# Expert weights of a two-layer MoE stack loaded as neighbouring rows per partition, with the fill of the modulation spread over single parts

## The chip, the cores and the metric

The kernel runs on one core of a Trainium2 chip. The metric is the device time of one execution in microseconds, from first instruction to last; less is better. Several executions are shown, and the median counts.

## What is computed

The reference chains two blocks on 256 tokens of width 1024, all in fp32. Cut to what matters:

```python
for l in range(2):                                   # first block
    x = x + 0.5 * swiglu(rmsnorm(x, norm_ffn1[l]), w_ffn1_in[l], w_ffn1_out[l])
    h = rmsnorm(x, norm_mix[l])
    x = x + mixing_sublayer(h, ...)                  # retention and forgetting attention, gated
    x = x + 0.5 * swiglu(rmsnorm(x, norm_ffn2[l]), w_ffn2_in[l], w_ffn2_out[l])
x = rmsnorm(x, norm_final)
...
for i in range(2):                                   # second block: x and 256 context tokens
    mod = silu(c) @ w_ada[i] + b_ada[i]              # also for c_ctx; shifts, scales, gates
    a = attention(x * (1 + sc1) + sh1)               # i == 0: window GQA, i == 1: differential
    x = layer_norm(ALPHA * x + g1 * a)
    h = x * (1 + sc2) + sh2
    s = sigmoid(h @ w_router)                        # 16 experts in 4 groups, top 2 of one group
    for e in range(16):
        y = (silu(h @ w_gate[e]) * (h @ w_up[e])) @ w_down[e]     # 1024 -> 512 -> 1024
        out = out + gates[:, e:e + 1] * y
    x = layer_norm(ALPHA * x + g2 * out)
```

Layer 0 of the second block routes 512 tokens (x and context), layer 1 only 256.

## The kernel before

The program is written by hand for each engine, in one order of stages: ffn0, mix0, ffn1, ffn2, mix1, ffn3 (the first block), then attention `qa`, `o0`, experts `m0` (4 tiles of 128 tokens), attention `qb`, `o1`, experts `m1` (2 tiles). Semaphores with named events (`pe.up(name)`, `q.wait_ge(*pe.at(name))`) tie the engines together.

**Weights.** A product in fp32 is made of three passes of PE over rounded halves: x_hi w_hi, x_hi w_lo, x_lo w_hi (`pe_gemm`, L334, L335, L336). `plan` cuts every weight into chunks of 1 MB (128 partitions x 2048 numbers) and each chunk into two parts of 128x1024. SP loads the chunks in program order into four buffers RAW (`load_chunks`, L300; `chunk_ap` gives the address). ACT rounds each part into HI (`hi_parts`, L268), DVE subtracts it from RAW into LO (`lo_parts`, L281, or L283 where a norm's gain is folded in), and five parts may be in flight. Both work four parts ahead of PE. A buffer is free for the next load once LO of both its parts is made.

In `chunk_ap` row k0*128 + k*128 + p of the weight goes to partition p ("(k p) c -> p k c"): a partition reads rows that lie 128 apart, each 512 columns or 2 KB in one packet. The x that is multiplied has the matching order, since PE turns blocks of 128 neighbouring columns.

**Experts.** In `pe_moe`, for each expert i: p of expert i-1 is turned, gate and up of expert i are multiplied (`a`, `b`, each 8 rows x 512 columns), the gathered x of i+1 is turned, and y of i-1 is made as two products of 512 columns from w_down, each by its own `pe_gemm` into its own PSUM bank. ACT makes silu(a) (L2036), and copies each y half out (L2049); DVE multiplies by b (L2244). POOL gathers the 128 tokens of an expert from HD by an indirect DMA (L2272); ACT's queue stores y to YD. The inputs h are made by `dve_modulate_folded` (L1342, L1344), two operations of 128x1024 for each tile of tokens, then stored to HD and turned for the router. Experts with over 128 tokens run again for the rest behind the loop (`pe_further` and its like): there PE multiplies RAW itself, unsplit (L1805, L1817). With these inputs two experts in each layer do.

**Fill.** The modulation `mod` needs w_ada, 96 parts for the whole program. Generators `pe_ada`, `act_ada`, `dve_ada` are stepped by `next(fill, None)` inside loops that have room: mix0 and mix1 (24 parts each) and the attention loop of qa (48 parts). One step brings two parts. In mix the loops have 5 steps in the retention part and 19 in and after the attention part, in qa there are 64 steps in the heads' loop (exp L1556) of which the first 32 work on scores of 512 columns and the last 32 on 256, with a copy on DVE (L1601) in every other step.

**Start.** For the first stage `act_ffn` and `dve_ffn` split the first weights (L537, L573) ahead of the norm; `act_norm` copies the turned x (L369) and squares x (L443).

## Time and profile before

| | before |
|---|---|
| runs shown, us | 2906.01, 2893.61, 2903.13 |
| median, us | 2903.13 |
| profiled execution: time, us | 2892.89 |
| profiled execution: span, us | 2891.1 |
| granted PE clock, mean | 0.916 |
| PE, PE weight loads, DVE, ACT busy | 89%, 70%, 61%, 50% |
| DMA moved | 575.90 MB, mean 199 GB/s |
| weight queue q1 | 249600 packets, 505.13 MB, 51.1% |

The shares are of the span. The span is what the profiler recorded from first to last instruction. PE is TensorE, DVE VectorE, ACT ScalarE, POOL GpSimd, SP the engine whose queue loads the weights. A share of a queue is the summed time of its packets over 16 DMA engines. The granted clock is a share of full speed (2.4 GHz): 1.00 or 0.50, or a mean of both over a stretch.

### The profile page before, as it was taken

To read this page: it belongs to the slowest core of one execution; us is meant where nothing else is said; L and a number is where in the kernel's file an instruction comes from. 1 tells how busy PE (TensorE), PEld (TensorE's weight loads), DVE (VectorE), ACT (ScalarE), POOL (GpSimd) and SP (SyncE) were. 2 spreads that over 40 slices of the span, in tenths; PEclk is the share of its full clock that TensorE was granted. 3 is DMA by queue.
4 is the path that set the end of the run, shared out by engine and by line. 5 is a ranking of instruction groups with operands and counts; after the bars stand their busy time and mean duration, and the time that the engine had idled before them with its cause. 6 is when DMAs were issued, how large, how long until landed. Compare 5 with 4: busy or idle time off the path is not lost. (4 is left out here: it accounts for less than half of the span.)

```text
span 2891.1 us, 30073 instructions
## 1 busy us (share of the span) xinstructions
PE 2573.7 (89%) x11670; PEld 2032.7 (70%) x11670; DVE 1757.0 (61%) x2527; ACT 1449.5 (50%) x2145; POOL 114.0 (4%) x118
## 2 busy tenths in 40 slices
PE   7999899999999989998989996999967977999953
PEld 6887777887887767886766664788846745888731
DVE  4555555555555555556356447798876366888812
ACT  5555645555555644554255311677732342777710
POOL 0001000000001000000000000000011000000000
PEclk9999989999999989998999766999968987999976
DMA  6664635665664535664255012899962203999952
GB/s 239 230 230 143 200 118 167 218 217 191 233 226 153 190 124 183 212 218 160 73 171 192 4 45 74 291 381 389 390 229 95 74 16 116 343 391 392 386 182 82
DMA packets 268314, 575.90 MB, mean 199 GB/s; under 512 B 14532, under 2 KB 23172, under 8 KB 268132
## 3 DMA queue, kind: packets, MB, share of 16 engines
q1 hardware_dynamic: 249600, 505.13, 51.1%
q10 hardware_dynamic: 11928, 44.49, 3.8%
q0 software_dynamic: 6624, 24.12, 2.3%
q8 instruction: 102, 1.67, 0.2%
q14 instruction: 60, 0.49, 0.1%
HBM read 526.31 MB, written 47.38 MB: 198 GB/s over the span
## 5 line engine op out<-in xcount | busy, mean ns | idle before, releaser
L281 DVE TENSOR_TENSOR LO<-RAW,HI 128x1024 fp32r<-128x1024 f32 x654 | 776.4, 1221 | 437.8 <-ACT HI L268 435.8
L334 PE MATMUL PS<-HI,FR 128*128 128x512 f32 (+2 forms) x2400 | 943.3, 393 | 62.7 <-DVE FR L373 29.1
L336 PE MATMUL PS<-HI,FR 128*128 128x512 f32 (+2 forms) x2400 | 929.8, 387 | 0.0
L335 PE MATMUL PS<-LO,FR 128*128 128x512 f32 (+2 forms) x2400 | 929.4, 387 | 0.0
L268 ACT ACTIVATE HI<-RAW 128x1024 fp32r<-128x1024 f32 x654 | 665.6, 1052 | 445.7 <-PE PS L336 322.1
L334 PEld LDWEIGHTS PS<-HI,FR 128*128 128x128 f32 x2400 | 460.9, 192 | 172.9 <-DVE FR L373 33.3
L283 DVE SCALAR_TENSOR_TENSOR LO<-RAW,SM,HI 128x512 fp32r<-128x512 f32 (+2 forms) x576 | 381.6, 708 | 310.9 <-ACT HI L268 310.9
L336 PEld LDWEIGHTS PS<-HI,FR 128*128 128x128 f32 x2400 | 460.4, 192 | 92.6
L335 PEld LDWEIGHTS PS<-LO,FR 128*128 128x128 f32 x2400 | 461.2, 192 | 86.0
L268 ACT ACTIVATE HI<-RAW,SM 128x512 fp32r<-128x512 f32 (+2 forms) x576 | 361.3, 681 | 292.0 <-PE PS L336 208.7
L369 ACT ACTIVATE FR<-PS 128x512 fp32r<-128x512 f32 x224 | 124.3, 586 | 197.4 <-PE PS L355 185.0
L355 PE MATMUL PS<-CN,SC 128*128 128x128 f32 x1056 | 169.3, 292 | 35.1 <-DVE SC L2486 16.9
L373 DVE TENSOR_TENSOR FR<-PS,FR 128x512 fp32r<-128x512 f32 x224 | 144.2, 674 | 57.7 <-ACT FR L369 57.4
L355 PEld LDWEIGHTS PS<-CN,SC 128*128 128x128 f32 x1056 | 135.6, 156 | 56.4 <-DVE SC L2486 20.2
L525 PE MATMUL PS<-HI,FR 128*128 128x512 f32 x352 | 137.3, 390 | 4.4 <-DVE FR L373 4.4
L526 PE MATMUL PS<-LO,FR 128*128 128x512 f32 x352 | 137.0, 389 | 0.0
L527 PE MATMUL PS<-HI,FR 128*128 128x512 f32 x352 | 137.0, 389 | 0.0
L355 PE MATMUL PS<-CN,HB 128*128 128x128 f32 x184 | 39.3, 384 | 73.6 <-DVE HB L1344 51.7
L1556 ACT ACTIVATE SC<-PS,SM 128x512 f32<-128x512 f32 (+1 forms) x64 | 37.2, 582 | 105.9 <-DVE SM L1609 105.9
L355 PEld LDWEIGHTS PS<-CN,HB 128*128 128x128 f32 x184 | 32.4, 203 | 82.3 <-DVE HB L1344 56.4
L667 PE MATMUL PS<-HI,CS 128*128 128x512 f32 x192 | 85.2, 444 | 3.1 <-DVE SC L1590 3.1
L668 PE MATMUL PS<-LO,CS 128*128 128x512 f32 x192 | 80.9, 421 | 0.0
(285 smaller groups left out, 1986.6 us busy)
## 6 DMA issues: line engine op xcount, KB each, us to landing
RAW<-in_w_ffn_in SPq DMA_DIRECT2D x88, 1024.0 KB, 5.2
RAW<-in_w_gate SPq DMA_DIRECT2D x68, 1024.0 KB, 8.3
RAW<-in_w_up SPq DMA_DIRECT2D x68, 1024.0 KB, 8.0
RAW<-in_w_down SPq DMA_DIRECT2D x68, 1024.0 KB, 8.7
RAW<-in_w_ada SPq DMA_DIRECT2D x48, 1024.0 KB, 5.1
RAW<-in_w_ffn_out SPq DMA_DIRECT2D x44, 1024.0 KB, 4.9
RAW<-in_w_in SPq DMA_DIRECT2D x44, 1024.0 KB, 5.1
YD<-CN ACTq DMA_DIRECT2D x24, 1024.0 KB, 5.0
```

The source lines that it names most:

```text
L268: e.activation(HI[:, j % NSPLIT, c], raw_of(j)[:, c], ACT.Copy, scale=1.0 if g is None else g).then_inc(*hi_done.up())
L281: e.tensor_tensor(LO[:, j % NSPLIT, c], raw_of(j)[:, c], hi, ALU.subtract).then_inc(*lo_done.up())
L283: e.scalar_tensor_tensor(LO[:, j % NSPLIT, c], raw_of(j)[:, c], g, hi, ALU.mult, ALU.subtract).then_inc(*lo_done.up())
L334: e.matmul(o, h, hi[:, j, :], start=first and k + j == 0, stop=False)
L335: e.matmul(o, h, lo[:, j, :], start=False, stop=False)
L336: x = e.matmul(o, ll, hi[:, j, :], start=False, stop=end)
L355: x = e.matmul(PS[b][:, k * P:k * P + P], s, ident, start=True, stop=True, is_transpose=True)
L369: e.activation(dst, turned(name, m), ACT.Copy).then_inc(*act.up(f"{name} hi"))
L373: e.tensor_tensor(dst, turned(name, m), hi.bitcast(F32), ALU.subtract).then_inc(*dve.up(f"{name} lo"))
L525: e.matmul(o, a, hh, start=first, stop=False)
L526: e.matmul(o, a, ll, start=False, stop=False)
L527: x = e.matmul(o, b, hh, start=False, stop=end)
```

## The change

It has four parts.

1. **Addresses.** For the router, gate, up and down weights `chunk_ap` gives partition p neighbouring rows ("(p k) c -> p k c"): four rows of 2 KB in gate and up, two rows of 4 KB in down, so 8 KB at a stretch. w_down is planned as two chunks of two full rows, and a new `pe_down` makes both halves of y for each row, in two banks that end together. ACT splits all four parts of w_down, then copies both halves out. The same addresses are used for the experts with over 128 tokens.
2. **Column order of the inputs.** So that the rows still meet their columns, the MoE inputs and p are written in the order of the weights' partitions: the operation reads x, gain and bias with a stride of 8 numbers (32 bytes), silu(a) and b with a stride of 4 (16 bytes), and writes one number behind the other.
3. **Fill.** The generators yield after each part and no longer after two: mix takes 24 steps (5 and 19), qa the first 48 of 64.
4. **Start.** The early split of the first weights in `act_ffn` and `dve_ffn` is gone; the norm comes first.

```diff
+ROW_RUNS = ("w_router_2", "w_gate_2", "w_up_2", "w_down_2")
...
+            if w[0] in ROW_RUNS:
+                return a.rearrange("(p k) c -> p k c", p=P)[:, k0:k0 + nk, c0:c0 + ncol]
             return a[k0 * P:(k0 + nk) * P, c0:c0 + ncol].rearrange("(k p) c -> p k c", p=P)
...
         def act_ffn(e, q, f):
             s = f"ffn{f}"
-            if f == 0:
-                hi_parts(e, q, 0)
             act_norm(e, q, s)
...
         def dve_ffn(e, q, f):
             s = f"ffn{f}"
-            if f == 0:
-                lo_parts(e, q, 0)
             dve_norm(e, q, s)
...
                             x.then_inc(*pe.up(f"used {m}"))
-                        if hk == 1:
-                            pe.also(f"{s} ada {l}{sec}{c}")
-                            freed[b] = [(act, f"{s} mod {l}{sec}{c}")]
-                        yield
+                            if hk == 1 and k + kk == 4:
+                                pe.also(f"{s} ada {l}{sec}{c}")
+                                freed[b] = [(act, f"{s} mod {l}{sec}{c}")]
+                            yield
...
                         for m in of[f"{s} ada {l}{sec}{c}{hk}"]:
                             lo_parts(e, q, m)
-                        yield
+                            yield
...
+        def as_rows(x, n):
+            return x.rearrange("p (q k) -> p k q", k=n)
+
+        def in_rows(x, n):
+            return x.rearrange("p (k q) -> p k q", k=n)
+
+        def dve_modulate_folded(e, q, s, stats, which, dsts, G, B, free, runs=False):
             for t in range(2):
                 g = 2 * which + t
+                o, x, gg, bb = dsts[t], stream(g), G, B
+                if runs:
+                    o, x, gg, bb = in_rows(o, 8), as_rows(x, 8), as_rows(gg, 8), as_rows(bb, 8)
...
-                e.scalar_tensor_tensor(dsts[t], stream(g), mv(g, 0), G, ALU.subtract, ALU.mult).then_inc(*dve.up())
+                e.scalar_tensor_tensor(o, x, mv(g, 0), gg, ALU.subtract, ALU.mult).then_inc(*dve.up())
...
+        def pe_down(e, q, name, w, xh, xl, banks):
+            for k0 in (0, 2):
+                for m in plan(name, w, k0, 2, 0, D, None):
+                    k = k0 + parts[m][1]
+                    hi, lo = halves_at(m)
+                    q.wait_ge(*lo_done.at(m))
+                    for h in range(2):
+                        if k == 0:
+                            pe_free(q, banks[h])
+                        o, hh, ll = PS[banks[h]][:, :], half_of(hi[:, 0, :], h), half_of(lo[:, 0, :], h)
+                        e.matmul(o, xh[:, k, :], hh, start=k == 0, stop=False)
+                        e.matmul(o, xh[:, k, :], ll, start=False, stop=False)
+                        x = e.matmul(o, xl[:, k, :], hh, start=False, stop=k == 3)
...
+                    yb = [pe_bank(q, f"{s} y {i - 1}{h}", rot) for h in range(2)]
+                    pe_down(e, q, f"{s} y {i - 1}", ("w_down_2", l, i - 1), *x_pT[(i - 1) % 2], yb)
...
+                    for m in of[f"{s} y {i - 1}"]:
+                        hi_parts(e, q, m)
                     for h in range(2):
-                        for m in of[f"{s} y {i - 1}{h}"]:
-                            hi_parts(e, q, m)
                         q.wait_ge(*pe.at(f"{s} y {i - 1}{h} 0"))
...
-                    e.tensor_tensor(x_p[i % 2], x_s[i % 2], PS[bank[f"{s} b {i}"]][:, :], ALU.mult).then_inc(
+                    e.tensor_tensor(in_rows(x_p[i % 2], 4), as_rows(x_s[i % 2], 4), as_rows(PS[bank[f"{s} b {i}"]][:, :], 4),
+                                    ALU.mult).then_inc(
```

How it moves instructions, at three places. First ACT at the start of the program (HI from RAW is the split, FR from PS the copies of the turned x, HB,SM from XL the squares), before:

```order
L412 ACTIVATE SM<-PS 128x48
L268 ACTIVATE HI<-RAW,SM 128x512 x10
L369 ACTIVATE FR<-PS 128x4x128 x4
L443 ACTIVATE HB,SM<-XL 128x1024 x2
L268 ACTIVATE HI<-RAW,SM 128x512 x6
```

and with the change:

```order
L416 ACTIVATE SM<-PS 128x48
L373 ACTIVATE FR<-PS 128x4x128 x4
L447 ACTIVATE HB,SM<-XL 128x1024 x2
L272 ACTIVATE HI<-RAW,SM 128x512 x16
L558 ACT_TABLE_LOAD
```

The ten splits that stood ahead of the copies and squares now follow them.

Second DVE in the loop of qa (LO from RAW is a part of the fill, the reduce of PS is a step's row maximum), before:

```order
L281 TENSOR_TENSOR LO<-RAW,HI 128x1024 x2
L1606 TENSOR_REDUCE SM<-PS 128x1
L1609 TENSOR_TENSOR SM<-SM 128x1
L281 TENSOR_TENSOR LO<-RAW,HI 128x1024 x2
L1601 COPY SC<-PS 128x512
L1606 TENSOR_REDUCE SM<-PS 128x1
L1609 TENSOR_TENSOR SM<-SM 128x1
```

and with the change:

```order
L285 TENSOR_TENSOR LO<-RAW,HI 128x1024
L1615 TENSOR_REDUCE SM<-PS 128x1
L1618 TENSOR_TENSOR SM<-SM 128x1
L285 TENSOR_TENSOR LO<-RAW,HI 128x1024
L1610 COPY SC<-PS 128x512
L1615 TENSOR_REDUCE SM<-PS 128x1
L1618 TENSOR_TENSOR SM<-SM 128x1
```

Each step now carries one subtraction of a part instead of two, and 48 steps have one instead of 24.

Third ACT in one expert of the loop (SC from PS at L2036 or L2063 is the silu, at L2049 or L2076 the copy of y), before:

```order
L2036 ACTIVATE SC<-PS 128x512
L268 ACTIVATE HI<-RAW 128x1024 x4
L369 ACTIVATE FR<-PS 128x512 x2
L268 ACTIVATE HI<-RAW 128x1024 x2
L2049 ACTIVATE SC<-PS 128x512
L268 ACTIVATE HI<-RAW 128x1024 x2
L2049 ACTIVATE SC<-PS 128x512
L2055 DMA YD<-SC 128x1024
```

and with the change:

```order
L2063 ACTIVATE SC<-PS 128x512
L272 ACTIVATE HI<-RAW 128x1024 x4
L373 ACTIVATE FR<-PS 128x512 x2
L272 ACTIVATE HI<-RAW 128x1024 x4
L2076 ACTIVATE SC<-PS 128x512 x2
L2082 DMA YD<-SC 128x1024
```

The last two splits stand ahead of the first copy of y; both copies are one behind the other.

## Rows read from the trace of the kernel before

**Rows 1.** The page: busy us of an engine (share of the span), and a queue's packets, MB, share

```profile
PE 2573.7 (89%) x11670; PEld 2032.7 (70%) x11670; DVE 1757.0 (61%) x2527; ACT 1449.5 (50%) x2145; POOL 114.0 (4%) x118
...
q1 hardware_dynamic: 249600, 505.13, 51.1%
```

**Rows 2.** Windows of expert loops: us, busy PE, PEld, DVE, ACT, POOL, PEclk, DMA, GB/s

```profile
1836.86:1855.44 18.58, 18.58 (x93) 15.63 (x92) 17.07 (x21) 15.19 (x18) 0.94 (x1) 1.00 0.96 330
1855.44:2101.39 245.95, 244.29 (x1191) 201.99 (x1190) 219.47 (x265) 193.28 (x234) 11.26 (x12) 1.00 1.04 385
2474.92:2493.06 18.14, 18.14 (x89) 15.18 (x88) 16.69 (x19) 15.20 (x18) 0.95 (x1) 1.00 1.01 366
2493.06:2737.17 244.11, 240.22 (x1143) 196.62 (x1142) 215.92 (x243) 193.40 (x235) 11.39 (x12) 1.00 1.04 386
```

**Rows 3.** Waits in m0, 1880 to 2090: engine, line, releaser, us, times, longest

```profile
ACT HI L268 <- DMA RAW<-in_w_down: 23.8, 23, 1.9
...
PEld PS L334 <- DVE LO L281: 4.5, 9, 0.9
```

**Rows 4.** Timeline of one step of qa: start, us, instruction, idle before it

```profile
1504.32 0.48 PE L667 MATMUL PS<-HI,CS 128*128 128x512 f32 x1
...
1504.47 0.69 ACT L1556 ACTIVATE SC<-PS,SM 128x512 f32<-128x512 f32 x1 [1.79 <-DVE SM L1609]
...
1506.02 0.39 PE L668 MATMUL PS<-LO,CS 128*128 128x512 f32 x1
...
1506.23 2.36 DVE L281 TENSOR_TENSOR LO<-RAW,HI 128x1024 fp32r<-128x1024 f32 x2 [1.79 <-ACT HI L268]
...
1508.51 0.69 DVE L1601 COPY SC<-PS 128x512 f32<-128x512 f32 x1
1509.11 0.68 DVE L1606 TENSOR_REDUCE SM<-PS 128x1 f32<-128x512 f32 x1
...
1510.02 0.69 ACT L1556 ACTIVATE SC<-PS,SM 128x512 f32<-128x512 f32 x1 [2.40 <-DVE SM L1609]
```

**Rows 5.** Timeline of the start

```profile
6.04 3.60 PE L355 MATMUL PS<-CN,XL 128*128 128x128 f32 x16 [1.82 <-DMA XL<-in_x]
10.53 6.69 ACT L268 ACTIVATE HI<-RAW,SM 128x512 fp32r<-128x512 f32 x10 [6.07 <-DMA RAW<-in_w_ffn_in]
...
17.13 2.04 ACT L369 ACTIVATE FR<-PS 128x512 fp32r<-128x512 f32 x4
...
21.18 0.77 PE L334 MATMUL PS<-HI,FR 128*128 128x512 f32 x1 [11.54 <-DVE SM L459]
```

**Rows 6.** DMA queues in m1, 2529 to 2746: packets, MB, share

```profile
q1 hardware_dynamic: 36723, 72.95, 91.0%
q10 hardware_dynamic: 1716, 6.24, 7.1%
```

**Rows 7.** Timeline, second expert with over 128 tokens in m1

```profile
2817.02 9.15 PE L1805 MATMUL PS<-RAW,SC 128*128 128x512 f32 x15 [2.37 <-DMA RAW<-in_w_up]
```

**Rows 8.** Instructions by line and shape, m0's modulation (1754 to 1775) and expert products

```profile
L1344 DVE SCALAR_TENSOR_TENSOR HB<-HB,SM,SC 128x1024 f32<-128x1024 f32 x4 | 5.1, 1285 | 0.1
...
L2244 DVE TENSOR_TENSOR SC<-SC,PS 128x512 f32<-128x512 f32 x14 | 9.5, 680 | 0.0
```

**Rows 9.** Busy by window, qa: steps 0 to 23, 24 to 31, 32 to 46, 47 to 62

```profile
1463.09:1586.35 123.26, 115.80 (x555) 81.27 (x554) 82.72 (x115) 74.89 (x123) 0.00 (x0) 0.94 0.60 192
1586.35:1607.26 20.91, 20.91 (x124) 13.92 (x122) 10.35 (x24) 8.27 (x21) 0.00 (x0) 1.00 0.21 85
1607.26:1633.53 26.27, 25.50 (x142) 17.12 (x141) 15.36 (x48) 11.35 (x42) 0.00 (x0) 0.95 0.00 1
1633.53:1677.16 43.63, 43.63 (x138) 27.93 (x138) 16.02 (x50) 13.52 (x45) 0.00 (x0) 0.50 0.00 1
```

**Rows 10.** Busy by window, mix0: first and later attention steps

```profile
338.00:369.00 31.00, 23.48 (x116) 17.85 (x115) 24.05 (x38) 20.36 (x39) 6.67 (x4) 0.93 0.74 248
369.00:398.00 29.00, 27.52 (x149) 21.21 (x148) 8.84 (x22) 8.04 (x28) 0.00 (x0) 0.78 0.11 37
```

More of the change, by code:

```diff
@@ L680, in act_ada @@
                             hi_parts(e, q, m)
-                        if hk == 1:
-                            q.wait_ge(*pe.at(f"{s} ada {l}{sec}{c}"))
-                            if (l, sec) == sections[0] and c < 2:
-                                for ev in stage_free(c):
-                                    q.wait_ge(*ev)
-                            else:
-                                q.wait_ge(*mod_out[c % 2].last())
-                            e.activation(stage[c % 2], PS[4 + c % 2][0:4, :], ACT.Copy).then_inc(
-                                *act.up(f"{s} mod {l}{sec}{c}"))
-                            q.wait_ge(*act.last())
-                            e.dma_start(MOD[l, sec, :, 512 * c:512 * c + 512], stage[c % 2]).then_inc(
-                                *mod_out[c % 2].up(f"mod {l}{sec}{c}", by=16))
-                        yield
+                            if hk == 1 and m == of[f"{s} ada {l}{sec}{c}{hk}"][-1]:
+                                q.wait_ge(*pe.at(f"{s} ada {l}{sec}{c}"))
+                                if (l, sec) == sections[0] and c < 2:
+                                    for ev in stage_free(c):
+                                        q.wait_ge(*ev)
+                                else:
+                                    q.wait_ge(*mod_out[c % 2].last())
+                                e.activation(stage[c % 2], PS[4 + c % 2][0:4, :], ACT.Copy).then_inc(
+                                    *act.up(f"{s} mod {l}{sec}{c}"))
+                                q.wait_ge(*act.last())
+                                e.dma_start(MOD[l, sec, :, 512 * c:512 * c + 512], stage[c % 2]).then_inc(
+                                    *mod_out[c % 2].up(f"mod {l}{sec}{c}", by=16))
+                            yield
         def dve_ada(e, q, s, sections):
@@ L1816, in one @@
                     for i in range(4):
[L1817 removed]
+                        x = e.matmul(PS[5 + h][:, :], x_p[1][:, P * i:P * i + P], RAW[:, i // 2, 1024 * (i % 2) + 512 * h:1024 * (i % 2) + 512 * h + 512],
                                      start=i == 0, stop=i == 3)
@@ L1901, in one @@
                 q.wait_ge(*more_pe.at(f"{s} ab 0"))
-                for h in range(2):
-                    e.dma_start(RAW[:, h, :].rearrange("p (k c) -> p k c", k=4),
-                                A["w_down_2"][l, k][:, 512 * h:512 * h + 512].rearrange("(k p) c -> p k c", p=P)).then_inc(
+                for i in range(2):
+                    e.dma_start(RAW[:, i, :].rearrange("p (k c) -> p k c", k=2),
+                                A["w_down_2"][l, k].rearrange("(p k) c -> p k c", p=P)[:, 2 * i:2 * i + 2, :]).then_inc(
                                     *more_w.up(by=16))
@@ L2202, in dve_moe @@
             for which in range(NT // 2):
-                dve_modulate_folded(e, q, s, f"o{l}", which, HBS, *o_fold[which], hidden_free(which))
+                dve_modulate_folded(e, q, s, f"o{l}", which, HBS, *o_fold[which], hidden_free(which), runs=True)
                 dve_hidden_T(e, q, s, (2 * which, 2 * which + 1))
@@ L2250, in dve_moe @@
                 if i:
-                    for h in range(2):
-                        for m in of[f"{s} y {i - 1}{h}"]:
-                            lo_parts(e, q, m)
+                    for m in of[f"{s} y {i - 1}"]:
+                        lo_parts(e, q, m)
             dve_further(e, q, l)
@@ L2307, in sp_moe @@
                 if i:
-                    for h in range(2):
-                        for m in of[f"{s} y {i - 1}{h}"]:
-                            load_chunks(e, q, m)
+                    for m in of[f"{s} y {i - 1}"]:
+                        load_chunks(e, q, m)
             sp_further(e, q, l)
```

21 lines of the change are left out of this document (10 added, 11 removed).

## The prediction, made before the changed kernel ran

> **What bounds the kernel now.** I read the page's busy times first, to see which engine could set the pace, then busy times by stage, then waits. PE is busy 89% of the span, and the weight queue q1 takes 51% of the DMA engines' time [rows 1]. That is an average over unlike stages, so each edit is priced in its own stage.
>
> In the **expert loops** the DMA share is 1.04 and 385 GB/s move, while PE is busy 244 of 246 us [rows 2]. (Shares above 1 only mean that no DMA engine ever rests.) Both limits lie within a few per cent of each other. The waits tell which is late: ACT's split waits 23.8 us in 210 us for w_down alone, DVE then waits for ACT, and only 4.5 us of it arrive at PE [rows 3]. So transfers are just slower than PE, and the buffers hide most of that. The windows of rows 2 begin at a silu (ACT, L2036) of the loop: the first one of each layer is one expert whose weights were fetched ahead, the second is 13 experts. So an expert takes 245.95/13 = 18.92 us in m0 and 244.11/13 = 18.78 in m1, but 18.58 and 18.14 with weights at hand.
>
> In the **attention of layer 0** (qa) while it carries the fill, and in the two mixing stages, a chain of ACT and DVE bounds: exp, split, subtract, reduce, next exp [rows 4]. At the **start** PE waits 11.5 us for its first weights and x [rows 5].
>
> **Start.** ACT splits ten halves of weights from 10.53, when the first chunk has landed, until 17.2, then the x copies (2.04) and the squares follow until PE begins at 21.18 [rows 5]. Afterwards the x copies can follow PE's turns, which end at 9.64, so they end near 10.2, and the squares, which now take the rest of 4.05 us, near 12.3. The first part's two halves are then split by 13.6 (0.67 each) and DVE's two subtractions, as long as the splits, done by 15.0; with gaps I take 15.7. Nothing else feeds PE, so 21.18 - 15.7 = **-5.4 us** (bounds -4.5 and -5.8). The squares take the place of the split as what PE waits for: they are late next.
>
> **The transfer of expert weights.** A packet grows from 2 KB to 8 KB. No 8 KB weight packet is in the trace. From below: packet size does nothing, q1 stays at 72.95 MB in 91.0% of 217 us = 369 GB/s [rows 6]. From above: q10, whose packets are almost twice as long (6.24 MB in 1716, 3.6 KB against 2.0), moves 6.24 MB in 7.1% = 405 GB/s [rows 6], and 8 KB might do a little more. An expert needs 6.29 MB of weights (3 x 1024 x 512 x 4 bytes) and 0.52 each of gathered input and stored output, 7.34 MB: 18.8 us at 390 GB/s, which is the period seen, and 18.1 at 405. I take 405, the nearest row. Then PE decides: the first, well-fed period ran 93 matmuls in 18.58 us, the other 1191 at that pace are 237.9 us, 18.30 each; in m1 89 in 18.14 make 1143 of them 233.0, 17.92 each [rows 2]. So the floor is 18.30 by PE in m0 and 18.1 by DMA in m1. Since two nearly equal limits interleave badly I take three quarters of the way in m0: 18.45, 13 x 0.47 = **-6.1 us** (0 to -8.1); in m1 18.08, 13 x 0.70 = **-9.1** (0 to -11.1).
>
> A rule speaks against this part. The Trainium skill, "DMA: Bandwidth & Descriptors", in its note on three bandwidth figures, says that a core's share of HBM (about 358 GB/s) binds transfers between HBM and SBUF, not the fabric. If so packets could not matter and both terms would be 0. The trace disagrees: the stage already moves 385 GB/s [rows 2], so the share as such is not what stops it.
>
> **Tail of the loops and the experts with over 128 tokens.** These two per layer are not split; PE waited 2.37 us for w_up before one [rows 7]. With faster loads I give each layer -1.5, and -0.5 each for the last y: **-4 us** (0 to -6). w_down's new plan keeps ACT's parts; both y copies (0.59 each) now stand together behind PE's last matmul, one copy later than before. Cover: ACT and DVE work four parts of six matmuls ahead, some 5 us; cost 0. Without that cover it is 0.59 x 28 = 16 us at most.
>
> **Strided vector operations.** Inputs are read with a stride of 32 bytes in 12 operations of 128x1024 (1.28 us each) and products with one of 16 bytes in 36 of 128x512 (0.68 us) [rows 8]. No strided operation of this sort is in the trace. From below: no cost. From above: half the rate, 12 x 1.28 = +15.4 us, since they stand between norm and router with PE waiting; the products lie in DVE's slack (219 of 246 busy, 16.9 of 18.9 per expert, 17.6 with them [rows 2]) and cost nothing so long as DVE stays below PE. I take **0**: the pace of these rows, 1024 elements in 1.28 us or 0.8 per ns, is that of one element at a time.
>
> The Trainium skill, "Advanced Engine Details and Errata", Memory Cachelines, says that SBUF has lines of 16 bytes and wants two hits on each, or there is a penalty. Every one of these reads breaks that. No run yet shows it; by the rule the upper end would hold.
>
> **Single parts of fill.** In qa one step carries two parts: from the exp at 1504.47, 1.76 until ACT has split one part and DVE may begin, 2.28 for two subtractions, 0.60 for a copy in every other step, 0.91 to the next exp at 1510.02 [rows 4]: 5.55 or 4.95. With one part it is 4.41 or 3.81, mean 4.11. Two thin steps thus cost more than one thick and one empty step (20.91/8 = 2.61 [rows 9]): 8.22 against 7.86. All 32 wide steps: 131.5 us against 144.2 now. But 16 narrow steps, now 1.75 each (26.27/15 [rows 9]), carry a part too: 3.35 or 3.7, so 56 against 28. Step 48 comes 15 us later. What is left, 15 steps, now runs at a clock of 0.50 in 2.73 us each (43.63/16); at full clock it is 1.75. The clock fell after a stretch of narrow steps without fill. If it holds for the 15 steps it gives 15 back, if not nothing: 0 to +15. I take **+5 us**, nearer to holding, since only 15 narrow steps are left without fill and now the clock held for 15 of them.
>
> In each mixing stage 12 of 24 parts move from the retention steps (5) and the first attention steps (7) to the later ones. There DVE is busy 24.05 of 31 us, and later 8.84 of 29 [rows 10]. A part is four matmuls on PE; in qa eight of them begin from 1504.32 to 1506.02, 0.243 apart, so a part is 0.97 us of PE [rows 4]. The parts that leave save between PE's work for a part and DVE's (a subtraction, 1.22); I count PE's, less a little that is hidden: 12 x 0.93 = 11.2 us. Later PE is busy 27.52 at a clock of 0.78, that is 21.5 at full clock; with 12 x 0.97 it is 33.1 at full clock and 42.5 at 0.78, against 29: +4.1 to +13.4. So -11.2 + 4.1 = -7 to -11.2 + 13.4 = +2 a stage; I take -4, since with work spread evenly the clock should fall less than now but hardly not at all. Twice that is **-8 us** (-14 to +4).
>
> **Sum**: -5.4 - 6.1 - 9.1 - 4 + 0 + 5 - 8 = -27.6. The profiled execution took 2892.89 us with a span of 2891.1; it is the fastest of those shown, 10 below the median 2903.13. On that median the forecast is **2875 us**, 1.0% faster.
>
> **The rivals.** (a) *The clock falls in the single-part fill*: slower. In narrow steps PE has 1.75 + 0.97 = 2.72 us of work in 3.5; now, with two parts, it is busier than that. If the granted clock is 0.50 there (1.2 GHz instead of 2.4), each step is PE's 5.4 us: 16 x 1.9 = +31 on top of +15, so qa costs +46, and the mixing stages +2 each. Against the sum below that is 41 and 12 more: -27.6 + 53 = +25, 2928 us. It decides where the clock of steps 32 to 47 is 0.50. For it: the clock of 0.50 behind narrow steps [rows 9]. Against: 0.94 with DVE-bound fill. Chance 0.09.
> (b) *Strided reads at half rate*, in the twelve modulations between the norm and the router: 2875.5 + 15.4 = 2891, chance 0.13. The trace has no such operation, so it speaks neither way; for it, each read then uses 4 bytes of every 32. The rule of the Trainium skill on 16-byte lines, above, is this rival.
> (c) *The packets do nothing* (the change doesn't do what it says), because HBM and not the packet's overhead sets 390 GB/s: both loop terms and 3 us of the tail's term go, 2875.5 + 15.2 + 3 = 2894, chance 0.12. For it: all queues together hold 380 to 390 GB/s in both loops [rows 2]. Against: in one window 3.6 KB packets pass at 405 and 2 KB packets at 369 [rows 6]. The note of the Trainium skill on the HBM share is this rival.
> (d) *All falls well*, PE is the bound where it can be and keeps its clock: PE's floor in both loops (-8.1, -11.1), full clock in mixing (-14), 0 in qa: -5.4 - 8.1 - 11.1 - 6 - 14 = -45, 2858, 0.20.
> The forecast itself, 2875 within 10, has 0.46.
>
> **Numbers.** A measurement of this kernel can tell about 0.5%, 14.5 us, from no change. Faster: the forecast, (d), and a part of (b) and (c), 0.72. Same: most of (b) and (c), 0.19. Slower: (a), 0.09. The range 2852 to 2902 takes in (b), (c), (d); (a) and part of the mishaps together are left out.
>
> **What would show it.** q1 loses 204 x 384 packets, to near 171,000. Right if: the first matmul with weights starts at 15 to 16; the silus of a loop stand 18.4 and 18.1 apart, with ACT's waits for w_down and w_up nearly gone; L1352 and L1354 still take 1.28 us; the exps of qa stand 4.1 apart for 32 steps, then 3.5, the 15 last at 1.75. Wrong if: the period stays at 18.8 (c), modulation takes 2.5 us (b), or the narrow steps take over 5 us (a). The step I trust least is the clock in qa.

## The result: slightly slower, and the profile after

| | before | after |
|---|---|---|
| median, us (9 runs each) | 2904.45 | 2911.83 |
| lowest, highest, us | 2893.61, 2911.06 | 2902.69, 2923.19 |
| ratio, with its 95% interval | | 1.0043, 1.0025 to 1.0062 |
| profiled execution, us | 2892.89 | 2902.69 |
| granted PE clock, mean | 0.916 | 0.919 |

The change costs 12 us by the ratio; the prediction had it 28 us faster. The profiled execution of each kernel is among the fastest of its kind, and 9.8 us lie between the two. The two medians lie 7.4 us apart, at the lower end of the ratio's interval (7 to 18 us).

One thing in the text ahead of the prediction has to be corrected: two experts in the whole program, both in m1, and not two in each layer, run again for more than 128 tokens. The trace of the kernel before has the matmuls of L1805 (64 records) only behind 2772 us, and the silu of these experts (L1833) twice in all.

The page of the changed kernel (busy time and share by engine; a queue's packets, MB, share) answers to [rows 1]:

```profile
PE 2569.3 (89%) x11670; PEld 2027.0 (70%) x11670; DVE 1778.5 (61%) x2527; ACT 1448.2 (50%) x2145; POOL 114.0 (4%) x118
...
q1 hardware_dynamic: 169472, 505.13, 49.5%
```

q1 has 80,128 packets fewer for the same bytes (249,600 before), so the change did what it says. The windows of the expert loops (length, then busy time of PE, PEld, DVE, ACT, POOL, then PEclk, DMA share, GB/s) answer to [rows 2]:

```profile
1844.56:1863.15 18.59, 18.59 (x94) 15.63 (x93) 17.43 (x21) 15.20 (x18) 0.94 (x1) 1.00 0.95 335
1863.15:2108.71 245.56, 243.34 (x1190) 201.95 (x1189) 223.76 (x264) 193.55 (x234) 11.24 (x12) 1.00 0.99 384
2485.62:2503.77 18.15, 18.15 (x90) 15.19 (x89) 16.81 (x19) 15.20 (x18) 0.95 (x1) 1.00 0.91 323
2503.77:2748.22 244.45, 239.58 (x1144) 197.04 (x1143) 219.92 (x243) 192.86 (x234) 11.38 (x12) 1.00 0.99 388
```

Look at the second and fourth row: 13 experts take 245.56 and 244.45 us, against 245.95 and 244.11. Nothing was gained. But the DMA share fell from 1.04 to 0.99. The queue row of this stretch of m0 (packets, MB, share) before

```profile
q1 hardware_dynamic: 41018, 81.48, 90.4%
```

and after:

```profile
q1 hardware_dynamic: 11136, 81.13, 85.3%
```

q1 moves 81.13 MB in 85.3% of 245.56 us, 387 GB/s while it is busy, against 367 before in the same loop (81.48 MB in 90.4% of 245.95 us). The packets are faster, and the loop does not use it. The waits of 210 us of m0, 1890 to 2100 (engine, line, releaser, total, times, longest), answer to [rows 3]:

```profile
ACT HI L272 <- DMA RAW<-in_w_down: 33.4, 22, 3.7
...
PEld PS L338 <- DVE LO L285: 2.6, 6, 0.6
ACT HI L272 <- DMA RAW<-in_w_up: 2.1, 3, 1.0
```

ACT's wait for w_up is nearly gone (2.1 us; it was 15.3 in the window of [rows 3]), but w_down is waited for longer, 33.4 us and up to 3.7 at a time instead of 23.8 and 1.9.

The start (timeline: start, length, instruction, idle before it) came as forecast, against [rows 5]:

```profile
10.07 0.60 ACT L373 ACTIVATE FR<-PS 128x512 fp32r<-128x512 f32 x1 [0.26 <-PE PS L359]
...
12.64 5.61 ACT L272 ACTIVATE HI<-RAW,SM 128x512 fp32r<-128x512 f32 x9
...
13.99 4.73 DVE L287 SCALAR_TENSOR_TENSOR LO<-RAW,SM,HI 128x512 fp32r<-128x512 f32 x7 [1.07 <-ACT HI L272]
...
15.55 0.76 PE L338 MATMUL PS<-HI,FR 128*128 128x512 f32 x1 [5.52 <-DVE LO L287]
```

PE begins at 15.55 and not at 21.18. In DVE's groups of m0's modulation the strided operations stand out, against [rows 8]:

```profile
L1354 DVE SCALAR_TENSOR_TENSOR HB<-HB,SM,SC 128x1024 f32<-128x1024 f32 x4 | 8.2, 2060 | 0.1
...
L1352 DVE SCALAR_TENSOR_TENSOR HB<-XC,SM,SC 128x1024 f32<-128x1024 f32 x2 | 4.1, 2074 | 0.2
```

```profile
L2271 DVE TENSOR_TENSOR SC<-SC,PS 128x512 f32<-128x512 f32 x13 | 14.1, 1082 | 0.0
```

2.07 us instead of 1.28, and 1.08 instead of 0.68: an operation with strided reads takes 1.6 times a plain one. L1352 reads x and gain with the stride, L1354 only the bias, and both take the same time, so here one strided input costs as much as two. The qa loop in windows, steps 0 to 23, 24 to 31, 32 to 47, and 48 to 63, answers to [rows 9]:

```profile
1458.13:1559.02 100.89, 95.96 (x475) 64.34 (x473) 57.97 (x94) 51.24 (x94) 0.00 (x0) 0.95 0.39 126
1559.02:1591.84 32.82, 31.30 (x161) 21.79 (x160) 19.15 (x33) 16.79 (x31) 0.00 (x0) 0.95 0.40 129
1591.84:1646.82 54.98, 47.07 (x198) 31.50 (x197) 32.89 (x66) 28.20 (x63) 0.00 (x0) 0.84 0.37 119
1646.82:1677.85 31.03, 30.50 (x127) 19.90 (x128) 15.23 (x48) 12.03 (x42) 0.00 (x0) 0.72 0.16 64
```

and one of its steps to [rows 4]: exp at 1500.28, the one subtraction at 1502.23, next exp at 1504.88.

```profile
1500.28 0.69 ACT L1565 ACTIVATE SC<-PS,SM 128x512 f32<-128x512 f32 x1 [1.60 <-DVE SM L1618]
...
1502.23 1.22 DVE L285 TENSOR_TENSOR LO<-RAW,HI 128x1024 fp32r<-128x1024 f32 x1
...
1504.88 0.69 ACT L1565 ACTIVATE SC<-PS,SM 128x512 f32<-128x512 f32 x1 [2.30 <-DVE SM L1618]
```

Most steps are 3.81 and 4.41 apart for the wide ones and 3.33 and 3.67 for the narrow ones, as forecast. The last 15 steps ran at a clock of 0.72 instead of 0.50, in 2.07 us each and not in the 1.75 named as a sign. That gave back 10.0 of the 15.6 us lost by step 48. Mix0 in the windows of [rows 10]:

```profile
338.00:369.00 31.00, 27.09 (x139) 20.53 (x139) 20.99 (x34) 15.62 (x34) 4.33 (x3) 0.89 0.50 162
369.00:398.00 29.00, 24.23 (x132) 19.26 (x131) 16.37 (x25) 15.52 (x30) 0.00 (x0) 0.94 0.47 155
```

DVE's work is spread more evenly now (20.99 and 16.37 us busy instead of 24.05 and 8.84), and the later window has a clock of 0.94 instead of 0.78.

Where the 9.8 us between the two traces came from, read at the same landmarks of both (difference of the change since the landmark before it): start and ffn0 -6.9, mix0 +2.1, ffn1 and ffn2 +0.1, mix1 0.0, ffn3 and the head of qa -0.2, qa's heads +5.7, from there to the first silu of m0 +5.0 (modulation in it 8 x 0.79 = +6.3), first expert +2.0, 14 experts -0.4, from m0 to m1's first silu +1.4 (modulation in it +3.0), first expert +2.0, 14 experts +0.4, the rest -1.3. Together they are the 9.8 us but for rounding.

The two +2.0 were in nobody's list. Behind gate and up of the first expert PE has nothing to do until DVE has the product p. This is the timeline before

```profile
1829.85 0.66 PE L355 MATMUL PS<-CN,SC 128*128 128x128 f32 x4 [0.75 <-DVE SC L2244]
...
1831.67 0.39 PE L336 MATMUL PS<-HI,FR 128*128 128x512 f32 x1
...
1832.12 0.39 PE L335 MATMUL PS<-LO,FR 128*128 128x512 f32 x1
```

and after:

```profile
1836.06 0.66 PE L359 MATMUL PS<-CN,SC 128*128 128x128 f32 x4 [1.12 <-DVE IDX L2248]
...
1837.32 0.53 PE L338 MATMUL PS<-HI,FR 128*128 128x512 f32 x1 [0.60 <-DVE FR L377]
...
1838.07 0.63 PE L340 MATMUL PS<-HI,FR 128*128 128x512 f32 x1
...
1838.92 0.63 PE L339 MATMUL PS<-LO,FR 128*128 128x512 f32 x1
```

PE's wait for p grew from 0.75 to 1.12 us with the strided product (the row names L2248, a 0.14 us operation that DVE ends 0.07 us behind the product), and soon after the matmuls follow each other at 0.43 and no longer at 0.23 us: the granted clock fell from its level of 2.4 GHz to that of 1.2 GHz for a few of them. In m1 the wait grew from 1.19 to 1.56 us, and the clock fell there too. Of the 2.0 us about 0.4 is the wait itself and 1.6 the clock.

All four first experts in the traces with the strided product and full PE work (this one and e3 below) have the fall. That the longer wait brings it is likely but not shown by itself: among the first experts of the twelve other traces with full PE work one, m1 of e13, has the same fall without any strided product, behind a wait of 1.25 us, and takes 15.49 us where the others take 13.9:

```profile
2471.32 0.66 PE L356 MATMUL PS<-CN,SC 128*128 128x128 f32 x4 [1.25 <-DVE SC L2245]
```

### The profile page after: what moved, and what is told of

It is laid out like the page before. It is cut to its first block and busy times, and to the rows that moved or that the text cites. A ratio compares the mean times of both kernels' runs of the same rounds, so it can differ in the third digit from the quotient of the medians.

```text
span 2900.9 us, 30075 instructions
## 1 busy us (share of the span) xinstructions
PE 2569.3 (89%) x11670; PEld 2027.0 (70%) x11670; DVE 1778.5 (61%) x2527; ACT 1448.2 (50%) x2145; POOL 114.0 (4%) x118
## 5 line engine op out<-in xcount | busy, mean ns | idle before, releaser
L338 PE MATMUL PS<-HI,FR 128*128 128x512 f32 (+2 forms) x2144 | 839.2, 391 | 50.5 <-DVE FR L377 22.7
L339 PE MATMUL PS<-LO,FR 128*128 128x512 f32 (+2 forms) x2144 | 829.0, 387 | 0.0
L340 PE MATMUL PS<-HI,FR 128*128 128x512 f32 (+2 forms) x2144 | 828.7, 387 | 0.0
L338 PEld LDWEIGHTS PS<-HI,FR 128*128 128x128 f32 x2144 | 412.4, 192 | 148.0 <-issue 33.2
L340 PEld LDWEIGHTS PS<-HI,FR 128*128 128x128 f32 x2144 | 411.8, 192 | 81.3
L339 PEld LDWEIGHTS PS<-LO,FR 128*128 128x128 f32 x2144 | 412.6, 192 | 77.1
L529 PE MATMUL PS<-HI,FR 128*128 128x512 f32 x352 | 137.3, 390 | 4.4 <-DVE FR L377 4.4
L531 PE MATMUL PS<-HI,FR 128*128 128x512 f32 x352 | 137.1, 389 | 0.0
L530 PE MATMUL PS<-LO,FR 128*128 128x512 f32 x352 | 137.0, 389 | 0.0
L1931 PE MATMUL PS<-HI,FR 128*128 128x512 f32 x256 | 104.5, 408 | 8.6 <-DVE FR L377 6.7
L1933 PE MATMUL PS<-HI,FR 128*128 128x512 f32 x256 | 101.8, 398 | 0.0
L1932 PE MATMUL PS<-LO,FR 128*128 128x512 f32 x256 | 101.3, 396 | 0.0
```

The source lines that it names most:

```text
L338: e.matmul(o, h, hi[:, j, :], start=first and k + j == 0, stop=False)
L339: e.matmul(o, h, lo[:, j, :], start=False, stop=False)
L340: x = e.matmul(o, ll, hi[:, j, :], start=False, stop=end)
L529: e.matmul(o, a, hh, start=first, stop=False)
L530: e.matmul(o, a, ll, start=False, stop=False)
L531: x = e.matmul(o, b, hh, start=False, stop=end)
```

## Experiments: each part by itself

All ratios are against the kernel before on the same chip in the same session. I first ran each part alone.

**e1: the start alone.**

```diff
 def act_ffn(e, q, f):
-    if f == 0:
-        hi_parts(e, q, 0)
     act_norm(e, q, s)
 def dve_ffn(e, q, f):
-    if f == 0:
-        lo_parts(e, q, 0)
     dve_norm(e, q, s)
```

> The kernel before with only the early split of the first weights removed. Theory A (each part's share read stage by stage from the two traces): first weight matmul at 15.4 instead of 21.2, 6 to 7 us faster, nothing changes behind ffn0. Rival B (the squares or a lower clock at the start give it back later): under 3 us.

Measured: 0.9979 (0.9959 to 0.9998), about 6 us faster; median 2896.66 against 2902.20. The trace has the first weight matmul at 15.28, 5.9 us earlier. Theory A holds in the trace; the interval (0.6 to 12 us) does not exclude rival B by itself, but e10 against e8 below shows the same 6 to 7 us once more. But the traced execution lost 4.6 us again in mix0, in code that is not touched; this is taken up with e12.

**e2: the fill alone** (the yields of `pe_ada`, `act_ada`, `dve_ada` after each part, in the kernel before).

> The kernel before with only the single-part fill. Theory A: qa +5 to +6, each mixing stage +1 to +2, together 7 to 9 us slower; exps of qa 4.4 and 3.8 apart, step 47 some 17 us late, the clock back at 1.00 before the last steps. Rival B (the fill is neutral, the loss after the change comes from elsewhere): within 3 us of before.

Measured: 1.0005 (0.9987 to 1.0023), median 2901.32 against 2902.20. The trace has what theory A says of qa: counted from its first exp, step 48 comes 14.3 us later, 8.1 of them are given back by the last, +6.2 in all. But the medians say no difference (the interval is -4 to +7 us). This expectation of 7 to 9 us was a miss; the reason is with e12 too.

**e3: the row runs and their strided operations alone.**

```diff
+            if w[0] in ROW_RUNS:
+                return a.rearrange("(p k) c -> p k c", p=P)[:, k0:k0 + nk, c0:c0 + ncol]
...
+                    o, x, gg, bb = in_rows(o, 8), as_rows(x, 8), as_rows(gg, 8), as_rows(bb, 8)
...
+                    pe_down(e, q, f"{s} y {i - 1}", ("w_down_2", l, i - 1), *x_pT[(i - 1) % 2], yb)
```

> The kernel before with only the row runs of the expert weights and the strided operations they need. Theory A: modulation 12 x 0.79 = +9.4 us, some 2 us at the first expert of each layer, expert loops unchanged at 18.9 and 18.8 per expert: 10 to 13 us slower. Rival B (the runs gain in the loops but other parts took it): 0 to 5 us slower.

Measured: 1.0032 (1.0007 to 1.0058), 9 us slower; median 2913.71 against 2902.20. The loss of the whole change is in this part. Periods 18.76 and 18.61 us: a little better than before, and than the changed kernel's own 18.89 and 18.80 with the same loop. So executions differ here. The four traces with the old loop (before, e12, e1, e2) have 18.92, 19.07, 18.96 and 18.79 in m0 and 18.78, 18.66, 18.72 and 18.71 in m1: one loop can differ by 0.3 us an expert, 4 us in 13.

**e4: the row runs without strides.**

```diff
-                    o, x, gg, bb = in_rows(o, 8), as_rows(x, 8), as_rows(gg, 8), as_rows(bb, 8)
...
-e.tensor_tensor(in_rows(x_p[i % 2], 4), as_rows(x_s[i % 2], 4), as_rows(PS[...], 4), ALU.mult)
+e.tensor_tensor(x_p[i % 2], x_s[i % 2], PS[...], ALU.mult)
```

> As e3, but the inputs of the experts and the products are written in plain column order, so rows and columns of the expert weights do not meet and the experts compute something else; the work is the same but for the strides. Theory A (the loops are not bound by the packets): 0 to 3 us faster than before, loop periods stay within 0.1 us of 18.9 and 18.8. Rival B (the strided product on DVE eats the gain of the packets inside the loop): 10 to 17 us faster than before, periods near 18.4 and 18.1.

Measured: 0.9982 (0.9963 to 1.0001), median 2898.47 against 2902.20. The windows of 13 experts:

```profile
1866.44:2108.83 242.39, 241.72 (x1191) 202.42 (x1190) 219.62 (x264) 193.99 (x235) 11.27 (x12) 1.00 0.99 390
2500.42:2744.52 244.10, 239.65 (x1143) 196.90 (x1142) 214.90 (x242) 192.59 (x235) 11.40 (x12) 1.00 0.99 387
```

242.39 us over 13 is 18.64, 244.10 over 13 is 18.78. So taking the stride away does not set the loop free, and rival B falls. Theory A is missed in m0 by a little (18.64, and 18.8 or more was expected) and holds in m1. The strides cost 0.0050 between e3 and e4, 14 us: 12 x 0.79 = 9.4 in the modulation and 2 x 2.0 at the first experts make 13.4. Packets of 8 KB gave some 5 us (0 to 11 by the interval), not all of it in the loops: six traces with row runs on the old buffers (after, e3, e4, e8, e10, e11) have a mean period of 18.74 and 18.69 us, the four with the old loop 18.93 and 18.72. That is 2.5 and 0.4 us in 13 experts.

## Experiments: what holds the expert loop

**e5: half the bytes.**

```diff
+                if chunks[n][0][0] in ("w_gate_2", "w_up_2", "w_down_2"):
+                    raw, src = raw[:, 0:2, :], src[:, 0:2, :]
                 e.dma_start(raw, src).then_inc(*raw_in[n % NRAW].up(by=16))
```

> The kernel before, but only the first two of four rows of each chunk of the loop's expert weights are loaded (same packets of 2 KB, half the bytes; the other rows are what the buffer held, so the experts compute something else). Theory A (PE and its handovers set the period, transfers do not): periods stay at 18.9 and 18.8. Rival B (transfers hold the loop, at a rate that 8 KB packets did not raise): periods fall to PE's own 18.3 and 17.9, 15 to 20 us faster over both loops.

Measured: 0.9913 (0.9886 to 0.9941). Windows of 13 experts:

```profile
1857.25:2098.01 240.76, 240.76 (x1190) 202.27 (x1189) 224.94 (x265) 197.59 (x234) 11.23 (x12) 1.00 0.70 225
2487.47:2722.87 235.40, 235.40 (x1142) 196.91 (x1141) 220.69 (x243) 197.67 (x234) 11.37 (x12) 1.00 0.71 230
```

PE is busy in every microsecond, and the periods are 18.52 and 18.11. That is PE's true floor in this program. The transfers did hold the loop, but the floor under them is higher than the 18.30 and 17.92 that I had worked out. The loops won 5.2 and 8.7 us, 13.9 together, less than the 15 to 20 expected of them; the whole ratio says 25 (17 to 33), and what the rest of it is was not looked into. The waits of PE's weight loads in m1 before, 2493 to 2737 us, are these, and in e5 none is left in either loop:

```profile
PEld PS L334 <- issue: 5.8, 12, 0.9
...
PEld PS L334 <- DVE LO L281: 3.7, 13, 0.7
```

("issue" is a wait whose end no releaser in the profile explains.) Together they are 9.5 us, near the 8.7 won; those with a named releaser alone are 3.7. In m0 it was 4.5 named and 1.1 not, for 5.2 won.

**e6 and e7: PE and DVE made light, with 2 KB and with 8 KB packets.**

```diff
+                    if chunks[parts[j][0]][0][0] in ("w_gate_2", "w_up_2", "w_down_2"):
+                        c = slice(0, 32)                          # lo_parts
...
-                        e.matmul(o, h, lo[:, j, :], start=False, stop=False)
+                        if w[0] not in ("w_gate_2", "w_up_2", "w_down_2"):
+                            e.matmul(o, h, lo[:, j, :], start=False, stop=False)
```

> The kernel before, but in the expert loops PE leaves out the product with LO and DVE makes only 32 columns of LO, so PE has 48 products for an expert instead of 72, DVE little, ACT 15.2 us, and transfers alone should set the period (the output is less exact). If transfers go at the rate seen (about 388 GB/s for 7.34 MB) the period is 18.5 to 18.9; if the ring of four buffers had held them back it is shorter, 17 to 18.

> The same as e6 on the row runs of 8 KB (with the early split and the fill of before). Theory A (8 KB packets are faster, but nothing in the full kernel waits for them): the period is 16.9 to 17.5, 1 us or more below e6. Rival B (HBM gives 388 GB/s whatever the packets): the same period as e6 within 0.2 us.

Measured: 0.9908 (0.9878 to 0.9938) and 0.9846 (0.9812 to 0.9880). e6, 13 experts:

```profile
1861.92:2105.23 243.31, 194.76 (x877) 137.04 (x876) 70.61 (x265) 192.93 (x235) 11.24 (x12) 0.99 1.05 392
2487.92:2730.01 242.09, 187.22 (x829) 129.51 (x828) 66.30 (x243) 192.80 (x235) 11.37 (x12) 1.00 1.05 392
```

and e7:

```profile
1874.26:2106.44 232.18, 187.61 (x878) 136.40 (x877) 75.70 (x264) 192.70 (x235) 11.24 (x12) 1.00 1.01 411
2491.28:2722.97 231.69, 184.00 (x830) 132.46 (x829) 71.37 (x242) 192.69 (x235) 11.37 (x12) 0.99 1.01 411
```

With PE busy only four fifths of the time, 2 KB packets need 18.72 and 18.62 us an expert at 392 GB/s, 8 KB packets 17.86 and 17.82 at 411. So the packets are 5% faster, as the row of 3.6 KB packets had promised, and rival B falls. Theory A's size was missed by a little: the periods are 0.9 and 0.8 below e6, where 1 or more was expected, and above the 16.9 to 17.5. e6 itself gave no sign of a limit by the buffers (17 to 18 would have been that sign); but DVE, which frees them, is busy only 71 of 243 us there. What the change gave (0 to 0.3 us an expert) is far from both floors, 18.52 and 18.11 by PE and 17.86 and 17.82 by the transfers. What I then took to stand between them is the ring of four buffers of 1 MB: a load starts only when DVE has made LO of both parts of the chunk four before it, and ACT splits only when the whole chunk has landed.

**e9: a finer ring** (on e8, below, whose loop is that of e4). The 32 KB of RAW become eight buffers of 128x1024, and each part is a load of its own.

```diff
-NRAW = 4
+NRAW = 8
-            chunks.append((w, k0, nk, c0, ncol, gain))
             for k in range(0, nk, ks):
                 mine.append(len(parts))
-                parts.append((n, k, min(ks, nk - k)))
+                parts.append((len(chunks), k, min(ks, nk - k)))
+                chunks.append((w, k0 + k, min(ks, nk - k), c0, ncol, gain))
```

> e8 with the same 32 KB of buffer cut into eight half-size buffers: every part is loaded by itself (512 KB, packets of 4 KB in the expert loops) and its buffer is free again when its own LO is made. Theory A (the ring of four 1 MB buffers couples transfers to DVE and PE, and eats what faster packets give): the periods fall below e8's 18.7 and 18.5 to about 18.5 and 18.2, though packets are smaller; 3 to 7 us faster than e8. Rival B (the handovers inside PE, ACT and DVE hold the loop): periods as in e8 or, by the smaller packets, up to 0.2 us longer.

```profile
1896.12:2137.89 241.77, 241.77 (x1190) 204.08 (x1189) 225.97 (x265) 197.36 (x235) 11.27 (x12) 1.00 1.01 393
2527.05:2763.47 236.42, 236.42 (x1142) 198.74 (x1141) 220.95 (x243) 197.63 (x235) 11.40 (x12) 1.00 1.02 403
```

PE is never idle: 18.60 and 18.19 an expert, PE's floor plus 0.08 for its strided turns, though the packets are only 4 KB. Theory A holds for the loop. In whole time it is 0.9972 (0.9957 to 0.9987), median 2895.89, against e8's 0.9985: the intervals overlap, so the gain over e8 is seen in the loops (5.7 us against e8's trace) and not in whole time. The traced execution, 2918.14 us, is the slowest of the thirteen; what it lost is in qa, taken up with e12. The edit does two things at once: a buffer comes free with each part, and a part can be split as soon as it has landed. Which of the two gave how much was not tried.

**e13: the finer ring on the kernel before, with its 2 KB packets.**

> The kernel before (2 KB packets, plain order) with the ring of eight half-size buffers alone. Theory A (transfers at the 2 KB rate need 18.7 us an expert, as e6 showed, and the ring lost the rest): the period comes down only to 18.7, 2 to 4 us faster in both loops; longer packets are needed for the rest. Rival B (the ring alone was the limit, packets do not matter): periods as in e9, 18.6 and 18.2.

Measured: 0.9964 (0.9946 to 0.9983), 10 us faster, with the planner's few lines changed and nothing else.

```profile
1866.07:2107.10 241.03, 241.03 (x1191) 202.50 (x1190) 223.47 (x265) 198.94 (x235) 11.27 (x12) 1.00 1.05 392
2498.23:2738.39 240.16, 238.23 (x1144) 196.75 (x1143) 218.59 (x243) 196.95 (x235) 11.40 (x12) 1.00 1.05 392
```

Periods 18.54 and 18.47. In m0 the ring alone brings the loop to PE's floor: there theory A's 18.7 was wrong, since e6 had the coarse ring in it too. In m1, where PE's floor is lower, the ring gives 0.31 us and the longer packets the other 0.28 (18.19 in e9). So ring and packets are both limits. By these traces the ring alone gives 8.9 us in the two loops; packets alone gave 3 (above), and on top of the ring 3.0 (e9 against e13).

## Experiments: the stride on PE, the fill, and the versions that win

**e8: PE reads the stride.** Inputs and products stay in plain order; the blocks that PE turns take every 8th or every 4th column.

```diff
+        def rows_of(src, n, at):
+            return [src.rearrange("p (q k) -> p k q", k=n)[:, at + k, :] for k in range(4)]
-                    b = pe_turn(e, q, f"{s} xT {i}{g}", blocks(x_g[i % 2], 4, 4 * g), rot)
+                    b = pe_turn(e, q, f"{s} xT {i}{g}", rows_of(x_g[i % 2], 8, 4 * g), rot)
```

> Row runs as in e3, but DVE writes inputs and products in plain order, and PE reads the columns with the stride when it turns them (all turned inputs and products of the experts). Computes what the reference does. Theory A (PE's turns do not mind the stride): like e4, 3 to 7 us faster than before. Rival B (PE pays for strided reads as DVE does): the turns of 128x128 take longer than 0.11 us each, 12 of them an expert, 10 us or more slower than e4.

Measured: 0.9985 (0.9967 to 1.0002), median 2895.23 against 2903.01. The turns in m0's loop before, and in e8:

```profile
L355 PE MATMUL PS<-CN,SC 128*128 128x128 f32 x140 | 19.4, 275 | 0.0
```

```profile
L359 PE MATMUL PS<-CN,SC 128*128 128x128 f32 x140 | 20.3, 281 | 0.0
```

6 ns more for each of them, and their weight loads, which PE overlaps with its matmuls, 202 ns instead of 147 each. Theory A holds. A first, well-fed expert takes 18.67 instead of 18.58. The order of the columns costs 16 x 0.09 = 1.4 us a layer on PE, and 6.7 on DVE.

**e10: e8 and the start's edit of e1.**

> e8 (row runs with PE reading the stride) and the start's edit. The two gains add: 8 to 12 us faster than before, about 2892. If only the clock's luck had made e1 and e8 look faster, it is within 4 us of before.

Measured: 0.9962 (0.9944 to 0.9981), median 2894.28. The gains add.

**e11: four parts of fill in a step of qa.**

```diff
-                        yield
+                        if s != "qa" or hk == 1:
+                            yield
```

> e10 with the fill of qa in 12 steps of four parts. By the step lengths (2.6 without a part, +1.5 for the first, +1.14 for each further one) 32 wide steps take 12 x 7.5 + 20 x 2.6 = 143 us instead of 144 to 147: 0 to 4 us faster than e10. Rival: four parts outrun the five in flight and the two chunks they need, and the step gets longer than 7.5 us, or the clock falls in the 20 thin steps: 5 us or more slower.

Measured: 0.9996 (0.9982 to 1.0009), 10 us slower than e10. The rival holds: step 24 comes 15 us later than in e10. The trace tells its two causes apart. The steps with four parts last 7.2 and 7.8 us, as the 7.5 said, so the parts did not outrun their buffers. But the wide steps without fill behind them last 5.18 us where e10 has 2.75, at a clock of 0.54 from 1554 to 1600 us: it was the clock.

**e14: e10 and the finer ring of e9.**

> Everything that helped, together: the start's edit, row runs with PE reading the stride, eight half-size buffers. Theory A: periods 18.6 and 18.2, start -6; 12 to 16 us faster than before, about 2889. Rival B (small loads cost elsewhere, as the 36 us in qa of e9's traced run suggest): no faster than e10.

Measured: 0.9942 (0.9919 to 0.9964), median 2886.19 against 2906.26: 17 us faster than before and the best of all. Its loops run at 18.60 and 18.19 as e9's. Against e10's ratio that is 6 us more, in another session; in the loops the two traces lie 5.2 us apart.

**e12: the kernel before again.**

> The kernel before once more, unchanged, for a second trace. Theory A (shifts of 2 to 5 us at the mixing stages and up to 8 in qa, seen in kernels whose code there is unchanged, come from where the clock's low phases fall, which differs between executions): some of the same landmarks stand 1 to 8 us off the first trace. Rival B (they follow from the code upstream): all landmarks within 0.5 us.

It took 2900.51 us. The last nine steps of the attention in mix0 and in mix1 are the same 128 matmuls in all kernels with the old fill. The first trace of before has mix0 (PEclk is the third number from the end)

```profile
369.20:393.62 24.42, 24.09 (x128) 18.55 (x128) 7.32 (x18) 6.78 (x24) 0.00 (x0) 0.75 0.13 44
```

the second trace of the same kernel has mix0 and mix1

```profile
369.75:392.42 22.67, 22.33 (x128) 17.12 (x127) 7.36 (x19) 6.78 (x24) 0.00 (x0) 0.81 0.15 47
1031.78:1060.84 29.06, 28.72 (x128) 22.07 (x127) 7.35 (x19) 7.00 (x24) 0.00 (x0) 0.61 0.12 37
```

and e1 has

```profile
363.62:392.69 29.07, 28.76 (x129) 22.41 (x130) 7.11 (x17) 6.99 (x25) 0.00 (x0) 0.62 0.12 37
1032.79:1055.46 22.67, 22.37 (x129) 17.46 (x130) 7.11 (x17) 6.77 (x25) 0.00 (x0) 0.82 0.15 47
```

22.67, 24.42 or 29.06 us for the same work, at a mean clock of 0.81, 0.75 or 0.61. The second trace of one kernel moved by -1.8 us in mix0 and +4.6 in mix1. Theory A holds. In qa the steps 24 to 47, unchanged in before, e4 and e9, show the same with larger sums:

```profile
1586.35:1636.15 49.80, 49.03 (x271) 32.69 (x270) 26.29 (x74) 20.58 (x65) 0.00 (x0) 0.95 0.09 37
```

```profile
1588.81:1646.73 57.92, 57.62 (x270) 37.79 (x271) 26.12 (x73) 21.47 (x66) 0.00 (x0) 0.79 0.08 33
```

```profile
1590.94:1676.44 85.50, 85.50 (x270) 55.98 (x271) 26.62 (x73) 22.51 (x66) 0.00 (x0) 0.50 0.05 18
```

49.80, 57.92 and 85.50 us at 0.95, 0.79 and 0.50. The traced execution of e9 lost its 36 us here, in steps without fill. Of thirteen traces with the old fill and 32 narrow steps without any, six lost 8 us or more there. The single-part fill carries work through 16 of these steps. So it pays 6 us in a good execution, as the first pair of traces showed, and saves some in a bad one, which fits e2's median of no difference; the second half of this sentence is argued from the traces and was not tried by itself.

## Why the prediction was wrong

- **Start**, -5.4 forecast: right. First matmul at 15.55 (15.7 said), -5.6 us, and -6 by e1's ratio.
- **Transfer of expert weights**, -6.1 and -9.1 forecast: this step failed, and it is the largest. Measured 0.4 us less and 0.3 more over 13 experts; by the means of six traces against four, -2.5 and -0.4. The rate was right: 8 KB packets go 5% faster (e7 against e6), I had said 405 against 390. Two sentences were wrong. "So the floor is 18.30 by PE in m0 and 18.1 by DMA in m1": I took PE's pace from the number of matmuls in the first period, but that number mixes products, turns and short ones, and some records can be missing; e5 has the floor at 18.52 and 18.11. And "I take three quarters of the way": two limits that lie 4% apart do not give the larger one, when a ring of four buffers ties them. The sizes themselves were near what there was to win (5.2 and 8.7 in e5; e14, with the finer ring, won 4.2 and 7.7). What failed is that faster packets alone would bring it. The waits had shown it: ACT waited 23.8 us for w_down alone, and PE got only 4.5 of that, so there were about 4.5 us to win in m0 and not 6.1, whatever the rate (e5, with no transfer late, won 245.95 - 240.76 = 5.2). What the faster packets saved stayed a wait, now at w_down, until e9 cut the buffers in two.
- **Tail**, -4 forecast: mis-sized twice. There are two late experts and not four, and behind the last expert of m1 the changed kernel won 1.3 us. Between m0 and m1 it won 1.6 besides what the modulation cost, and how much of that is the last y is not known.
- **Strides**, 0 forecast (0 to +15.4): this step failed too. The sentence "the pace of these rows, 1024 elements in 1.28 us or 0.8 per ns, is that of one element at a time" took the pace of a plain read as proof that a line of several numbers does not help it. Measured 2.07 us, 1.6 times, +9.4 for the modulations. Strides of 16 and of 32 bytes cost the same factor, 1.59 for p and 1.61 for the inputs. The rule of the Trainium skill ("Advanced Engine Details and Errata", Memory Cachelines) was right in direction: at both strides each read has a line of its own. It gives no size; that "the upper end would hold" was my addition, and the factor is 1.6 and not 2. I had given it a chance of 0.13, on no row at all. The +4 at the two first experts was in no term: I had said that the products cost nothing "so long as DVE stays below PE", which is true of the 14 later experts and not of the first, where PE waits for p.
- **Fill in qa**, +5 forecast: right in its trace (+5.7), step by step up to step 48. The clock of the last steps came back only in part (0.72, 2.07 us a step), which gave 10.0 us back, as the term had taken. In the medians it is not seen.
- **Mixing**, -8 forecast: measured +2.1 and 0.0. The steps became shorter as worked out (in mix0 exp 6 came 7.2 us earlier, counted from the first), but the 12 parts behind took it back. The traces of single executions cannot size such a term: the same steps vary by 6 us with the clock. Nor can e2's medians: with the fill in qa the forecast was -3, and the interval is -4 to +7.
- **Rivals**: (b) came true at 9.4 of its 15.4 us; (c) came true in nearly all of its price but not in its reason, since the packets are faster and the ring kept it from PE; (a) and (d) did not come. Each rival was priced alone, and the range left out two mishaps at once. By the prediction's own prices (b) and (c) together make 2875.5 + 15.4 + 18.2 = 2909 us, near the 2911.83 measured; but (b)'s price was too high and other terms made up for it, so part of that nearness is luck. The note on the HBM share in the Trainium skill ("DMA: Bandwidth & Descriptors") does not hold here, where one core runs: e7 moves 411 GB/s, above its figure of about 358.

Between the forecast of -27.6 and the +9.8 of the two traces lie 37.4 us: 15.2 in the loops, 13.4 in the strides and first experts, 10.1 in mixing, and -1.3 in all the rest. Put together from measured terms: -6 start, 0 loops, -1 tail, +13.4 strides and first experts, 0 to +6 fill gives +6 to +12; the ratio says 12. The single parts' ratios (-6, +1.5, +9) add to +5; the 7 us between that and 12 are within their intervals of 5 to 7 each.

## What to carry to other kernels

When an engine and its transfers both take about the whole period, price a faster transfer by all the waits that reach the bounding engine, those without a named releaser too (here 5.6 us of 246 in m0 and 9.5 of 244 in m1, for 5.2 and 8.7 that were there), not by the rates, and ask what ties the two: loads and buffers of half the size were worth 10 us here, packets four times as long about 5. A change of column order belongs on the operation that reads it for almost nothing, here PE's turns (6 ns each) and not DVE (0.4 to 0.8 us each). And before a term of a few us is read from two traces, look whether untouched stretches of the same code agree between them.

## What was not expected of the hardware

- DVE reads fp32 at a stride of 16 or 32 bytes 1.6 times slower than in a row (128x1024: 2.07 against 1.28 us; 128x512: 1.08 against 0.68), whether one input is strided or two, and PE's turns of 128x128 take the same stride for 6 ns (281 against 275; their overlapped weight loads 202 against 147).
- The same 128 matmuls took 22.67, 24.42 or 29.06 us, and one stretch of qa 49.8, 57.9 or 85.5, by the clock granted in that execution.
- Waits of PE that grew by 0.37 us (0.75 to 1.12 in m0, 1.19 to 1.56 in m1) were followed by a fall of the clock from 2.4 to 1.2 GHz that cost 1.6 us more, four times what the wait itself did. Once (m1 of e13) it fell so without the growth.
- Wide attention steps without fill took 5.18 us behind twelve steps with four parts each (e11, clock 0.54), and 2.75 behind twenty-four with two each (e10).
